# Hybrid decoder trunk: the gates are summed before mixer 1's norm columns, and mixer 1's weight sums are stored from ACT's queue

## What is computed

```
mod = silu(c) @ ada_w + ada_b          # 6 x 1024: shift1 scale1 gate1 shift2 scale2 gate2
h = rmsnorm(x, norm1_g) * (1 + scale1) + shift1
x = x + gate1 * hybrid_mixer(h)        # SSD heads and chunked gMLP heads, one w_in, one w_out
h = rmsnorm(x, norm2_g) * (1 + scale2) + shift2
x = x + gate2 * conv_gated_ffn(h)      # up-projection, causal conv of width 3, silu gate, down
out = rmsnorm(x, final_g)
```

## Time and profile before

| | us |
|---|---|
| median of 3 runs | 2803.24 |
| lowest, highest | 2801.07, 2805.23 |
| the profiled execution | 2800.92 |
| its span | 2799.2 |
| TensorE busy | 2709.3 |

### The profile page before, as it was taken

The page is one execution under the profiler, slowest core; times in us unless marked ns, Lnnn a source line. Parts: engine busy times, 40 slices in busy tenths (PEclk is TensorE's granted clock), DMA queues, the critical chain, the costliest instruction groups (busy, mean ns, idle before and its releaser), DMA issues.

```text
span 2799.2 us, 33835 instructions
## 1 busy us (share of the span) xinstructions
PE 2709.3 (97%) x12427; PEld 2214.0 (79%) x12427; DVE 1825.6 (65%) x2598; ACT 994.0 (36%) x1505; POOL 1046.6 (37%) x723
## 2 busy tenths in 40 slices
PE   7999889899999999999999999999999999999998
PEld 6777768677887888877878888888888788887886
DVE  6788765658567666558787667456655855545767
ACT  3544223321143333334444321143223433334333
POOL 2344340455236777744480110001102544444230
PEclk9999999999999999999999999999999999999999
DMA  9677676999955566664447767687676344445656
GB/s 383 235 249 296 221 287 204 335 345 327 317 199 181 192 210 207 200 242 138 159 138 265 256 210 250 204 276 239 220 237 231 104 128 126 127 124 196 220 169 221
DMA packets 262001, 620.49 MB, mean 222 GB/s; under 512 B 26725, under 2 KB 84553, under 8 KB 257739
## 3 DMA queue, kind: packets, MB, share of 16 engines
q1 hardware_dynamic: 261174, 618.08, 64.6%
q10 hardware_dynamic: 662, 0.24, 0.0%
HBM read 466.57 MB, written 151.66 MB: 221 GB/s over the span
## 4 chain that ended last, share of the span: by engine, by line
PE 76%; DVE 8%; DMA 6%; issue 3%; POOL 2%; SPq 2%; ACT 1%; DVEq 0%; ACTq 0%; POOLq 0%
PE main L1984 29%; PE pair L2254 15%; PE main L2254 14%; PE pair L2274 6%; PE main L2274 5%; DMA w_split_scratch<-w_hl 2%; PE pair L2121 2%; DMA t_up_scratch<-tb 1%; POOL w_hl L717 1%; PE pair L2146 1%; POOL tb L728 1%; DVE a_lo L1605 1%; DMA tb<-in_ff_up_dram 1%; PE pair L2106 1%; PE pair L2113 1%
## 5 line engine op out<-in xcount | busy, mean ns | idle before, releaser
L717 POOL TENSOR_TENSOR w_hl<-w_raw,w_hl 128x512 fp32r<-128x512 f32 x532 | 760.6, 1434 | 915.1 <-ACT w_hl L817 902.4
L817 ACT ACTIVATE w_hl<-w_raw 128x512 fp32r<-128x512 f32 x532 | 332.6, 630 | 830.9 <-PE main L2254 168.4
L1984 PE MATMUL main<-w_hl,h_hi 128*128 128x512 f32 x1536 | 491.3, 401 | 9.6 <-DMA w_hl<-w_split_scratch 7.2
L1984 PEld LDWEIGHTS main<-w_hl,h_hi 128*128 128x128 f32 x1536 | 283.7, 188 | 84.1 <-issue 16.6
L1984 PE MATMUL main<-w_hl,h_lo 128*128 128x512 f32 x768 | 300.2, 391 | 0.0
L728 POOL TENSOR_TENSOR tb<-tb,tb 128x512 f32<-128x512 f32 x132 | 201.3, 1525 | 184.1 <-DMA tb<-in_ff_up_dram 179.4
L754 POOL TENSOR_TENSOR pre_hl<-pre_raw,pre_hl 128x512 fp32r<-128x512 f32 x35 | 53.4, 1528 | 563.8 <-ACT pre_hl L841 563.8
L1984 PE MATMUL main<-h_hi,w_hl 128*128 128x512 f32 x768 | 250.8, 401 | 6.6 <-ACT stage L896 5.0
L2254 PE MATMUL pair<-s_hi,w_hl 128*128 128x512 f32 x736 | 235.7, 393 | 2.3 <-POOL w_hl L717 2.3
L2274 PE MATMUL main<-w_hl,a_hi 128*128 128x512 f32 x704 | 219.0, 392 | 7.6 <-DVE a_lo L1605 4.0
L1605 DVE TENSOR_TENSOR a_lo<-g,a_hi 128x512 fp32r<-128x512 f32 x132 | 160.2, 1222 | 97.7 <-ACT a_hi L1067 97.1
(11 more groups left out here) (287 smaller groups left out, 5079.8 us busy)
## 6 DMA issues: line engine op xcount, KB each, us to landing
w_hl<-w_split_scratch SPq DMA_DIRECT2D x312, 512.0 KB, 4.4
w_split_scratch<-w_hl SPq DMA_DIRECT2D x104, 512.0 KB, 6.7
w_raw<-t_up_scratch SPq DMA_DIRECT2D x176, 256.0 KB, 2.7
w_raw<-in_ff_up_dram SPq DMA_DIRECT2D x132, 256.0 KB, 3.7
tb<-in_ff_up_dram SPq DMA_DIRECT2D x88, 256.0 KB, 4.2
t_up_scratch<-tb SPq DMA_DIRECT2D x88, 256.0 KB, 5.6
g_scratch<-c_val SPq DMA_DIRECT2D x44, 512.0 KB, 4.0
g<-g_scratch SPq DMA_DIRECT2D x40, 512.0 KB, 7.3
```

The costliest lines, as they stand in the source:

```text
L717: nc.gpsimd.tensor_tensor(w_lo[:, g % RING, :], w_raw[:, g % RING, :], w_hi[:, g % RING, :].bitcast(F32), ALU.subtract).then_inc(w_lo_ok, 1)
L817: nc.scalar.activation(w_hi[:, g % RING, :], w_raw[:, g % RING, :], ACT.Copy).then_inc(w_hi_ok, 1)
L1984: ins = T.matmul(main[i], a, w, start=first and p == 0, stop=last and p == 2)
```

## The change

The gates take the place of shift2 and scale2 in the early ring (tiles 8 to 15, both gates in one transfer of 1 MB), and shift2 and scale2 come late, as eight transfers of 1 MB (`col_load`) and eight products of 2048 columns (`col_sum`). The row matmuls move to the end of unit 23, the row adds with them; the one-column matmuls move behind unit 83, `mod_columns(1)` behind the norm of block 1. Tiles 12 to 15 are issued at units 8, 11, 14 and 17 and not in the prologue; on VectorE tile 12 is summed behind dt_first, 13 behind dt_rest, 14 and 15 behind the second conv stage. The residual tiles of block 0 wait for the fourth mod_col. The stores of mixer 1's weight sums are issued by ACT at the same unit numbers in its own program, and SP keeps the loads.

```diff
-        ADA_RING, ADA_FIRST, HF0, ADA_PE = 12, 4, 2, 2
+        ADA_RING, ADA_FIRST, HF0, ADA_PE = 12, 8, 2, 2
-        gate_rows, _ = fixed("gate_rows", [1, 2 * D], F32, r_at + 80 * KB)
+        gate_rows, _ = fixed("gate_rows", [1, 2 * D], F32, x2_at)
+        col_spare, _ = fixed("col_spare", [P, 2 * D], F32, r_at + 48 * KB)
...
-        GATE_AT = (22, 34, 42, 50, 58, 70, 80, 85)
+        GATE_TILES = {8: 12, 11: 13, 14: 14, 17: 15}
+        COL_AT = {20: 1, 28: 0, 40: 2, 48: 3, 56: 4, 68: 5, 78: 6, 84: 7}
+        GATES_SUMMED = 2 * KD - ADA_PE
...
+            def col_load(k):
+                if k == 0:
+                    sp.wait_ge(gate_mm, 4)
+                elif k == 1:
+                    sp.wait_ge(ada_summed, KD + 3 - ADA_PE)
+                else:
+                    sp.wait_ge(ada_summed, GATES_SUMMED + k)
+                src = ada_w[0, k * P:(k + 1) * P, 3 * D:5 * D]
+                if k == 1:
+                    sp.dma_start(col_spare[:], src).then_inc(ada_in[5], 16)
+                else:
+                    sp.dma_start(mod_sum[:, 2:4, :].rearrange("p m d -> p (m d)"), src).then_inc(ada_in[4 + k % 2], 16)
...
-                        if n == at + 4:
+                        if b == 0 and n == at + 4:
                             t_store(t)
...
-                if b == 0 and n in GATE_AT:
-                    for m in (2 * GATE_AT.index(n), 2 * GATE_AT.index(n) + 1):
-                        gate_load(m)
-                if b == 0 and n == OUT + 12:
-                    sp.wait_ge(y_tr, KD)
+                if b == 0 and n in GATE_TILES:
+                    ada_load(GATE_TILES[n])
+                if b == 0 and n in COL_AT:
+                    col_load(COL_AT[n])
+                if b == 0 and n == 20:
+                    sp.wait_ge(mod_col, 3)
...
-                if b == 0 and n == OUT + 20:
+                if b == 0 and n == 30:
                     sp.wait_ge(gate_ok, 4)
...
                         if b == 0:
-                            sp.wait_ge(gate_mm, 4)
+                            sp.wait_ge(mod_col, 4)
...
+            def t_stores(n):
+                while t_next[0] in T_OF[1] and T_AT[1][t_next[0]] + 4 <= n:
+                    t = t_next[0]
+                    t_next[0] += 1
+                    act.wait_ge(t_add, 4 * t + 4)
+                    for which, holds in enumerate((T2, T4, T3, T1)):
+                        dst = tu_d[t // 2, holds, t % 2] if t < 2 * QN else td_d[holds, t - 2 * QN]
+                        act.dma_start(dst, tb[t_set(t)][which][:]).then_inc(t_st[t_set(t)], 16)
+
+            def beside_split(b, n):
+                if b == 1:
+                    t_stores(n)
...
+            def col_sum(k):
+                dst = mod_sum[:, 0:2, :].rearrange("p m d -> p (m d)")
+                piece = col_spare[:] if k == 1 else mod_sum[:, 2:4, :].rearrange("p m d -> p (m d)")
+                dve.wait_ge(ada_in[4 + k % 2], 16 * (k // 2 + 2))
+                if k:
+                    dve.wait_ge(ada_summed, GATES_SUMMED + k)
+                    V.scalar_tensor_tensor(out=dst, in0=piece, scalar=c_act[:, k:k + 1], in1=dst,
+                                           op0=ALU.mult, op1=ALU.add).then_inc(ada_summed, 1)
+                else:
+                    dve.wait_ge(gate_stored, 16)
+                    V.tensor_scalar(dst, piece, c_act[:, k:k + 1], None, ALU.mult).then_inc(ada_summed, 1)
...
-            for i in range(KD, KD + 5):
+            for i in range(KD, KD + 4):
...
-                        for i in range(KD + 5, 2 * KD):
-                            ada_sum(i)
+                        ada_sum(KD + 4)
...
                         dt_rest()
+                        ada_sum(KD + 5)
...
+                    if b == 0 and j == 1:
+                        ada_sum(KD + 6)
+                        ada_sum(KD + 7)
+                        dve.wait_ge(bias_in, 32)
+                        for m in range(4):
+                            dve.wait_ge(gate_mm, m + 1)
...
+                if b == 0:
+                    col_sum(5)
                 gate_y(1)
...
-                        if b == 0 and (j, k) == (2, 2):
-                            pe.wait_ge(ada_summed, 2 * KD - ADA_PE)
-                            mod_column(1, range(KD), aux[0])
+                        if b == 0 and (j, k) == (2, 7):
+                            pe.wait_ge(ada_summed, GATES_SUMMED)
+                            pe.wait_ge(ws_ok, 2)
+                            pe.wait_ge(acs_t_ok, 1)
+                            for m in range(4):
+                                T.matmul(aux[m][0:1, :], ones, mod_sum[:, 2 + m // 2, (m % 2) * W:(m % 2 + 1) * W],
+                                         start=True, stop=True).then_inc(gate_mm, 1)
...
-                        if b == 0 and j == 0 and k == 15:
+                        if b == 0 and j == 0 and k == 11:
                             pe.wait_ge(y_lo_ok, KD)
-                            pe.wait_ge(ada_summed, 4 * KD - ADA_PE)
...
+                            pe.wait_ge(ada_summed, GATES_SUMMED + KD)
+                            mod_column(range(KD), aux[0])
```

More of the change, by code:

```diff
@@ L1387, in mixer @@
                                             tri[:].unsqueeze(1).broadcast_to([P, 4, P]), ALU.mult).then_inc(ws_ok, 1)
+                    if b == 0 and j == 1:
[4 more added lines that the diff above has]
+                            dve.wait_ge(gate_mm, m + 1)
+                            row = gate_rows[0:1, m * W:(m + 1) * W]
+                            V.tensor_tensor(row, aux[m][0:1, :], row, ALU.add).then_inc(gate_ok, 1)
                     if b and j == 0:
@@ L1392, in mixer @@
                             finish_scale(0, y20_ok)
-                    if b == 0 and j == 2:
-                        gate_sums(0)
                 def heads(ap):
@@ L1458, in mixer @@
                     if b == 0 and cc < NT - 1:
-                        gate_sums(cc + 1)
+                        if cc == 0:
+                            col_sum(0)
+                        col_sum(cc + 1)
                 rms_rstd(NT)
@@ L1469, in mixer @@
                 if b == 0:
-                    gate_sums(NT)
+                    col_sum(NT)
                 for t in range(NT):
@@ L1512, in mixer @@
                 if b == 0:
-                    gate_sums(5)
+                    col_sum(6)
                 for k in range(KD):
@@ L1564, in mixer @@
                 if b == 0:
-                    gate_sums(6)
+                    col_sum(7)
                 if b % 2 == 0:
@@ L1568, in mixer @@
                 if b == 0:
-                    gate_sums(7)
-                    dve.wait_ge(pro_dma, 48)
-                    for m in range(4):
-                        dve.wait_ge(gate_mm, m + 1)
-                        row = gate_rows[0:1, m * W:(m + 1) * W]
-                        V.tensor_tensor(row, aux[m][0:1, :], row, ALU.add).then_inc(gate_ok, 1)
+                    mod_columns(1, slice(0, KD), aux[0], two_parts(col_b, R_AB + 2 * KD, slice(0, KD)), R_N2, 3)
                 if b == 0:
@@ L1934, in _, with mod_column @@
             ones = tri[:, P - 1:P]
-            def mod_column(n, ks, bank):
+            def mod_column(ks, bank):
                 for k in ks:
@@ L1940, in mod_column @@
                         m = part * KD + k
-                        last = T.matmul(bank[:, m:m + 1], mod_sum[:, 2 * n + part, k * P:(k + 1) * P], ones,
+                        last = T.matmul(bank[:, m:m + 1], mod_sum[:, part, k * P:(k + 1) * P], ones,
                                         start=True, stop=True)
@@ L1965, in _ @@
             pe.wait_ge(ada_summed, KD - ADA_PE)
-            mod_column(0, range(4), main[3])
-            mod_column(0, range(4, KD), main[2])
+            mod_column(range(4), main[3])
+            mod_column(range(4, KD), main[2])
             def weights_in(b, n):
@@ L2085, in chunk_scores @@
                         pe.wait_ge(silu_done, b * CONVS + (KX + 2))
-                        pe.wait_ge(ready, 3)
+                        pe.wait_ge(gate_ok, 4)
                         pe.wait_ge(ws_ok, 2)
@@ L2202, in mixer @@
                             y_transpose(range(4, KD))
-                        if b == 0 and j == 0 and k == 15:
+                        if b == 0 and j == 0 and k == 11:
                             pe.wait_ge(y_lo_ok, KD)
-                            pe.wait_ge(ada_summed, 4 * KD - ADA_PE)
-                            for m in range(4):
-                                T.matmul(aux[m][0:1, :], ones, mod_sum[:, m // 2, (m % 2) * W:(m % 2 + 1) * W],
-                                         start=True, stop=True).then_inc(gate_mm, 1)
+                            pe.wait_ge(ada_summed, GATES_SUMMED + KD)
+                            mod_column(range(KD), aux[0])
                         if b % 2 == 0 and j == 1 and k in (1, 9):
                             if b == 0 and k == 1:
-                                pe.wait_ge(gate_ok, 4)
```

(1 more changed line is left out.)

57 lines of the change are left out of this document (20 added, 37 removed).

## The result

| | before | after |
|---|---|---|
| median, us | 2802.15 (4 runs) | 2787.37 (4 runs, 2783.23 to 2788.27) |
| the profiled execution | 2800.92 | 2788.11 |
| its span | 2799.2 | 2786.4 |

What follows compares the result with a forecast made beforehand. TensorE, busy 97% of the span, was taken as the bound, so only its waits and half-clock stretches could yield. Gains of 11 + 19 + 0 = 30 us gave a 2773 us median, range 2762 to 2786.

Steps and rivals of the forecast that it cites:

- Part 1: Start to the first chunk: early waits and half clock go, 11 us gained, bounds 7 and 13.
- SP will wait longer ... hidden: Chunks: SP's longer wait for col_sum(4) ahead of unit 68 costs nothing, as TensorE takes that unit only at 301.
- Part 2: Chunks and gMLP, 151 to 336: products take the same time, y_ok comes slightly later, 0.4 us lost.
- Cost nothing: Start, unit 28: SP's wait for gate_mm is covered by loaded units and the SiLU wait; without cover 1 to 3 us.
- Part 3: Output product, 336 to 397: its long waits and gate matmuls go, 19.5 us gained, 19 after the 0.4; bounds 9 and 20.
- at about 345: Sign, output product: the half clock behind the one-column matmuls would appear at about 345 us.
- unit 89 ending at 367: Sign, end of the output product: unit 89 would end at 367 us, from 397 - 30.
- Part 4: Mixer 1: moving eighty stores to ACT's queue changes nothing, 0 us, since transfers bound it; range -9.9 to +8.
- C: Rival: the first stretch gains only 7 us and mixer 1 loses 4 on ACT; 2781 us, chance 0.15.
- F: Rival: ACT issues stores late, SP holds up weights, 12 waits of 3.3 us in mixer 1; slower, 2813, chance 0.03.
- B: Rival: loads pass stores on the other queue, mixer 1's 9.9 us of waits go too; 2763 us, chance 0.14.
- the forecast is wrong if these waits double: Sign, mixer 1: waits for split weights stay about 10 us, SP's landing waits above 49; doubling would refute the forecast.

Runs made afterwards that it cites:

- e3: The changed kernel with four late column loads moved two units later, to units 42, 50, 58 and 70; 2781.79 us, 0.9920 of the kernel before.
- e4: The changed kernel with mixer 1's stores back on SP's queue and four late column loads two units later; 2777.5 us, 0.9904 of the kernel before.
- e1: The changed kernel with only mixer 1's stores put back on SP's queue; 2779.95 us, 0.9911 of the kernel before.
- e6: The changed kernel with mixer 1's stores issued from GpSimd's queue behind each tile's fourth sum; 2776.42 us, 0.9910 of the kernel before.
- e8: The changed kernel, stores still on ACT, with mixer 1's tile loads one unit later in SP's order; 2788.1 us, 0.9941 of the kernel before.
- e9: A second run of e4, unchanged; 2776.07 us, 0.9903 of the kernel before.

## Why the prediction was wrong

- **The reading of the bounds** held: the waits named in mixer 0 went, and TensorE's idle time there with them.
- **Part 1** came out at 9.3 for 11 with the mechanism right but for one wait. "TensorE, at 116.7, waits 3 to 5 us": it got there at 121.6 and waited 1.8, because of 4.21 us at unit 19 and the slow clock behind it (0.57 in 103.77:107.30). The split of that unit stands on ACT behind a SiLU whose conv VectorE finished at 100.1 (the split ran at 101.6, the low part to 103.7). The kernel before has the same order, its split at 113.4, but there the 2.8 on da_t and the 4.84 of one-column matmuls covered it; the change took both away. The gate matmuls came at 123.34, 1.7 behind the latest of the forecast (119.6 to 121.6); the two sums took 6.37, 3.19 each, near the upper of the two prices, and began 2 us late, since wsT waited 2.84 for TensorE's transposes.
- **Part 2** failed: -0.4 forecast, -7.2 measured. The step was "SP will wait longer ... hidden". It asked whether TensorE has its weights in time, and it has: the waits for w_hl don't rise. But a split waits for its store, and behind the split on ACT stand dex, bc_tok and the copies v_sb: what the prediction had said of yT_hi in the kernel before, not applied to the chunks. And part 2 priced one of SP's six stalls for column sums (30.9 us in all). e3 and e4 show the part due to the loads at units 40 to 68; "Cost nothing", said of SP's wait for gate_mm, is another, 1.53 us at bc_tok in unit 29. The product in front of gate_y(1), forecast at 0.4, left TensorE waiting 1.13 for y_sb. The rest of the 7.2, some 1 us, is not traced to a cause.
- **Part 3** was right: 20.3 for 19.5, all waits of the output product gone, the half clock behind the one-column matmuls where the count put it (353.4:360.3 at 0.51; the sign "at about 345" didn't follow that count). The sign "unit 89 ending at 367" took the whole 30 off, against the 377.4 of its own count; counted back from 421.51 by the 46.9 us between 397.0 and 443.93, it was 374.6. In ten of the eleven other profiles with this output product the part gives 21.9 and not 20.3, above the upper bound of 20.
- **Part 4** failed too: 0 taken of a range from -9.9 to +8, and the cost was 8.3 by the marks, 9 by e1. The choice went by the busy share of 0.95 in 560:665, which is 0.95 after too. But the price fell outside that window, in the waits at 500 to 524 and 700 to 705 and the slow clock behind them, and at 494 to 497 the DMA engines ran dry while SP stood. The step that failed is that the 49.2 of landing waits "stays, because t_load still waits for t_st": it took the wait's existence for its length. SP no longer stands for the sums (31.5 us), so it is sooner at t_load, and the last store lands 8.8 us behind the first one's issue for 7.7 in e1; the landing waits became 69.3, and TensorE's waits for weights went from 9.9 to 16.8, two of them over 4 us. The other half of the bound, +8 from stores that ACT issues late, named the right sum for a reason that the traces don't bear out: ACT was 0.90 us behind the sums, as SP is in e1. And no term was there for the clock, though the earlier trace rows had it for every long wait of mixer 0.
- **The rivals.** C had the right place for half of the miss, with 4 in place of 8 us, and part 1 above its 7. F had the end of the chain right (late landing, SP holds the weights) and its start wrong, since the issue was not late behind the sums; its price of 3.3 us on each of 12 waits was four to five times too high: the landing waits rose by 20, of which 8 to 9 reached TensorE. B's gain didn't come. No rival had a loss in the chunks beside one in mixer 1, though both are SP standing in a queue that everything passes. The sign "the forecast is wrong if these waits double" didn't show either: they went from 9.9 to 16.8 and from 49.2 to 69.3, and the clock behind the long ones did the rest.
- **The Trainium skill** (DMA: Bandwidth & Descriptors, section "Issuing engines are not separate DMA queues") says that another issuing engine saves only the issuing. The runs agree in that no queue beat SP's beyond its interval (e1 and e6: 0.9911 and 0.9910); by that rule the part would be 0, and on ACT it was a loss, for which the rule has no term.

## What to carry to other kernels

A transfer that is moved to a compute engine's queue is issued in that engine's order: ask what it waits for, what stands behind it there (xdec and v_sb in e8), and who waits for its landing. Then time the whole lap of its buffer, not the issue alone: here the issue was as prompt as before and the landing 1.1 us slower. When a wait is taken from the queue that issues everything, ask what it held back; here it had put the stores ahead of the weights, and most of the wait came back under another name. Where a ring of splits hangs on stores, check each stall of the loading queue against the small operations that stand behind the splits, not only against the weights of TensorE.

## What was not expected of the hardware

The clock's part in a stall. Behind waits of TensorE of 4.2 to 5.4 us (those that end at 103.77, 504.54 and 705.35 in the changed kernel) the granted clock was at 0.54 to 0.57 over the 3.5 to 6.5 us read, so waits of 4.35 and 5.41 us cost 7.3 and 6.9 with the clock. Behind the eleven short waits for weights of before, 9.9 us in sum and none over 1.9, it stayed at 1.00. In between, the length of the wait doesn't decide: the clock was at 0.51 for a while behind waits of 1.96 (e3), 2.27 (before, on v_sb, ending at 665.57), 2.35 (changed) and 2.54 (e1), and at 1.00 behind 2.39 (e1, ending at 641.79) and 2.73 (e9, ending at 640.45). The one in the kernel before:

```profile
666.60:670.10 3.50, 3.50 (x20) 3.50 (x19) 3.50 (x8) 0.00 (x0) 0.00 (x0) 0.51 0.91 267
```

And GpSimd issued four stores in 2.2 us on average (539 ns for most), ACT in 2.4 (1.8 to 3.1), SP in 2.4 (1.8 to 2.9, e1): no engine is cheaper by much at the issuing itself.
